# Sums of squares of eight norms: one f32 product with ones against two fp32r products of a rounded part and a rest

## The reference

```python
def rms_norm(x, g):
    xf = x.astype(jnp.float32)
    y = xf * lax.rsqrt(jnp.mean(xf * xf, axis=-1, keepdims=True) + EPS) * g.astype(jnp.float32)
    return y.astype(x.dtype)
```

## Time and profile before

| | |
|---|---|
| median of three executions | 3236.54 us |
| the profiled execution: its time | 3235.9 us |
| the profiled execution: its span | 3234.1 us |
| TensorE (PE) busy | 3172.7 us, 98% |
| TensorE weight loads (PEld) | 2582.4 us, 80% |
| VectorE (DVE) busy | 1799.1 us, 56% |
| ScalarE (ACT) busy | 1143.2 us, 35% |
| GpSimd (POOL) busy | 438.8 us, 14% |
| DMA engines, mean share | 27% |
| mean granted clock of TensorE | 0.997 of 2.4 GHz |

### The profile page before, as it was taken

One profiled execution on the slowest core, in us unless ns is written; L12 is line 12 of the kernel. 1 busy time (PEld: TensorE's weight loads), 2 busy tenths in 40 slices (PEclk: granted clock), 3 DMA queues, 4 the chain that ended last, 5 costly groups with the idle time before them and its releaser, 6 DMA issues. The chain is left out here.

```text
span 3234.1 us, 41361 instructions
## 1 busy us (share of the span) xinstructions
PE 3172.7 (98%) x15706; PEld 2582.4 (80%) x15706; DVE 1799.1 (56%) x1935; ACT 1143.2 (35%) x1330; POOL 438.8 (14%) x339
## 2 busy tenths in 40 slices
PE   8899999999999999999999999999999999999998
PEld 6678888877788888888877888888888876888887
DVE  7775535459653455544586654345444576664344
ACT  4463322249432222322353433223322343533221
POOL 2001000110100025000153120003000154120002
PEclk9999999999999999999999999999999999999999
DMA  4212232232123224222221122324223221122322
GB/s 157 80 48 76 100 104 91 103 112 72 66 91 104 91 93 116 104 95 103 86 84 53 66 91 84 111 81 126 103 91 104 78 92 66 53 91 91 104 88 81
DMA packets 46599, 293.44 MB, mean 91 GB/s; under 512 B 5888, under 2 KB 6272, under 8 KB 18336
## 3 DMA queue, kind: packets, MB, share of 16 engines
q1 hardware_dynamic: 44496, 286.97, 25.9%
q0 software_dynamic: 2000, 5.05, 1.0%
HBM read 289.24 MB, written 2.10 MB: 90 GB/s over the span
## 5 line engine op out<-in xcount | busy, mean ns | idle before, releaser
L1899 DVE TENSOR_TENSOR w_lo<-w_raw,w_hi 128x2048 fp32r<-128x2048 f32 (+1 forms) x284 | 666.7, 2348 | 242.1 <-ACT w_hi L1460 241.9
L900 PE MATMUL ps<-xg_hi,w_hi 128*128 128x512 f32 x1920 | 749.7, 390 | 2.2 <-DVE w_lo L1899 2.2
L900 PE MATMUL ps<-xg_hi,w_lo 128*128 128x512 f32 x1920 | 747.1, 389 | 0.0
L900 PE MATMUL ps<-xg_lo,w_hi 128*128 128x512 f32 x1920 | 747.0, 389 | 0.0
L1460 ACT ACTIVATE w_hi<-w_raw 128x2048 fp32r<-128x2048 f32 (+1 forms) x286 | 541.2, 1892 | 476.5 <-PE ps L900 359.5
L900 PE MATMUL ps<-hid_hi,w_hi 128*128 128x512 f32 x1216 | 473.4, 389 | 0.0
L900 PE MATMUL ps<-hid_lo,w_hi 128*128 128x512 f32 x1216 | 473.1, 389 | 0.0
L900 PE MATMUL ps<-hid_hi,w_lo 128*128 128x512 f32 x1216 | 473.1, 389 | 0.0
L900 PEld LDWEIGHTS ps<-xg_hi,w_hi 128*128 128x128 f32 x1920 | 360.4, 188 | 79.2 <-issue 4.8
L900 PEld LDWEIGHTS ps<-xg_lo,w_hi 128*128 128x128 f32 x1920 | 360.4, 188 | 75.9 <-issue 1.4
L900 PEld LDWEIGHTS ps<-xg_hi,w_lo 128*128 128x128 f32 x1920 | 360.4, 188 | 75.3
(11 more groups left out here) (362 smaller groups left out, 3933.1 us busy)
## 6 DMA issues: line engine op xcount, KB each, us to landing
w_raw<-up_dram SPq DMA_DIRECT2D x120, 1024.0 KB, 4.9
w_raw<-in_dram SPq DMA_DIRECT2D x42, 1024.0 KB, 4.9
w_raw<-down_dram SPq DMA_DIRECT2D x32, 1024.0 KB, 4.8
w_raw<-down_dram SPq DMA_DIRECT2D x32, 768.0 KB, 4.2
w_raw<-down_dram SPq DMA_DIRECT2D x32, 640.0 KB, 3.9
w_raw<-out_dram SPq DMA_DIRECT2D x14, 1024.0 KB, 4.9
w_raw<-out_dram SPq DMA_DIRECT2D x8, 768.0 KB, 4.2
w_raw<-memk_dram SPq DMA_DIRECT2D x4, 1024.0 KB, 4.9
```

What stands on the lines that cost most here:

```text
L900: last = pe.matmul(to, (w_hi, w_lo)[wp][:, q, t:t + P], parts[xp], start=(k == 0 and m == 0), stop=(k == p.ktiles - 1 and m == 2))
L1899: dve.tensor_tensor(w_lo[:, q, 0:w], w_raw[:, q, 0:w], w_hi[:, q, 0:w].bitcast(F32), ALU.subtract)\
```

## The change

GpSimd gets two more instructions behind each of the eight sums: a copy of `ssq` into an fp32r tile `ssq_hi`, which rounds, and a subtraction that leaves the rest in `ssq_lo`. `ssq_lo` lies on the bytes of `ssq`, and `ssq_hi` on those of `sq`. TensorE waits for the second of them and makes two fp32r products with ones into the same bank in place of the one f32 product. Two semaphores are added; `split_before(n)` counts how many such splits came before norm n. The first norm, the middle one and the last one stay as they were.

```diff
+def split_before(n):
+
+    return n - 1 - (n > gained(MID + 1))
...
+    ssq_lo = at("ssq_lo", [S], F32R, c[0])
     ssq = const("ssq", [S])
+    ssq_hi = at("ssq_hi", [S], F32R, c[0])
     sq = const("sq", [S])
...
+        def split_sums(n):
+
+            pool.wait_ge(ssq_ready, DT * (n + 1))
+            pool.tensor_copy(ssq_hi[:], ssq[:]).then_inc(ssq_h, 1)
+            pool.wait_ge(ssq_h, split_before(n) + 1)
+            pool.tensor_tensor(ssq_lo[:], ssq[:], ssq_hi[:].bitcast(F32), ALU.subtract).then_inc(ssq_split, 1)
...
                     pool.tensor_tensor(ssq[:], ssq[:], tmp[:, b % 2, :], ALU.add).then_inc(ssq_ready, 1)
+                split_sums(n)
...
-                    squares(n, wait, DT - 1 if p.next_norm == NORMS - 1 else DT)
+                    last = p.next_norm == NORMS - 1
+                    squares(n, wait, DT - 1 if last else DT)
+                    if not last:
+                        split_sums(n)
...
-                pe.matmul(ps[:, 7, :], ones[:], ssq[:], start=True, stop=True).then_inc(ss_mm, 1)
+                pe.wait_ge(ssq_split, split_before(n) + 1)
+                pe.matmul(ps[:, 7, :], ones[:].bitcast(F32R), ssq_hi[:], start=True, stop=False)
+                pe.matmul(ps[:, 7, :], ones[:].bitcast(F32R), ssq_lo[:], start=False, stop=True).then_inc(ss_mm, 1)
```

More of the change, by code:

```diff
@@ L336, in program @@
     ssq_ready = sem("ssq_ready")
+    ssq_h = sem("ssq_h")
+    ssq_split = sem("ssq_split")
     xsq_done = sem("xsq_done")
```

## The result

The changed kernel takes 3254.02 us (median of six executions, 3252.07 to 3257.26) against 3235.84 us (six, 3235.24 to 3236.61): 18.2 us more, a ratio of 1.0056 with a 95% interval of 1.0045 to 1.0067. The forecast was 3249.6 us, 13.1 more.

The account below looks back on a forecast made before the run. TensorE, busy 98%, was taken to bound the kernel; 12.05 + 1.83 - 0.82 = +13.1 us gave 3249.6 us. The 8-in-10 range was 3243 to 3252, the forecast's own 3247.5 to 3251, with chance 0.70.

Parts of the forecast that it names:

- TensorE saves 0.41 us a norm: At each of eight norms, two fp32r products replace one f32 product: 0.41 us saved, 3.3 us in all without waits.
- GpSimd's two instructions: Behind each sum, undisturbed: copy 0.69 us and subtraction 1.28 us, 2.13 us together with gaps.
- The copy is held behind `w_lo`: In five norms GpSimd's copy waits for VectorE's `w_lo`, lasting some 2.6 us, from 335.1 to 337.8 in up1_0_0.
- rival 1: Only GpSimd's subtraction is held by `w_lo`, not the copy: +1.65 us in five norms, +7.0 us, 3243.6 us; chance 0.13.
- The five alike: Norms up1_0_0, in1_1, in2_0, in2_1, up2_1_0_0: product 2.82 us late, less 0.41 saved, +2.41 each, +12.05 us.
- up1_1_0: At this norm the subtraction is held behind `w_lo`, so the product starts 2.24 us late, less 0.41: +1.83 us.
- the other two: Norms up2_0_1_0 and up2_1_1_0: GpSimd finishes before TensorE asks, no wait, -0.41 us each, -0.82 together.
- Whoever comes second is held: Two-input VectorE and GpSimd instructions don't run side by side; the later waits, then needs its time less some 0.13 us.
- The race in up1_1_0: GpSimd's subtraction is issued 0.1 us behind `w_lo` and held, +1.83 us; if it won, -0.24 us.
- Costed at nothing: Later root, reciprocal, evictions, slab splits and table loads add no time; a lost cover costs at most 4 us once.
- Rival 3: TensorE's later waits in attention and gated stages, 15.9 us, shrink and give the stalls back: not slower; chance 0.05.
- what TensorE is spared or made to wait there moves the end of the program one for one: Around up1_0_0's norm TensorE has no gap, at 0.227 us a slot and full clock, so delays count in full.

Follow-up runs that it names:

- e6: Kernel before with GpSimd's sums written as fp32r and two fp32r products of that one tile, no split or added wait: 3233.36 us, ratio 0.9989.
- e8: Changed kernel with the rounding copy on ScalarE instead of GpSimd, subtraction still on GpSimd: 3249.94 us, ratio 1.0038 to the kernel before.
- after: First profile of the changed kernel itself, compared with the kernel before: profiled execution 3253.88 us, median 3254.02 us.
- e9: The changed kernel, unaltered, profiled a second time: 3254.90 us.
- e10: The changed kernel, unaltered, profiled a third time: 3250.46 us.
- e2: Changed kernel plus throwaway fp32r products on TensorE ahead of its wait for the split at six norms: 3249.80 us, ratio 1.0043 to the kernel before.
- e5: Changed kernel with copy, subtraction and wait kept, but the old single f32 product of the unsplit sum: 3255.69 us, ratio 1.0063 to the kernel before.
- e4: Changed kernel with token_rms 24 products later in four norms and both in2 norms back to unsplit f32: 3238.89 us, ratio 1.0009 to the kernel before.
- e3: Changed kernel with VectorE starting the neighbouring w_lo only after GpSimd's subtraction in six norms: 3237.65 us, ratio 1.0004 to the kernel before.
- e7: Changed kernel with w_lo after GpSimd's subtraction and token_rms 6 products later, both in six norms: 3233.99 us, ratio 0.9991 to the kernel before.

## Why the prediction was wrong, step by step

- **TensorE saves 0.41 us a norm**: right; e6 has 0.34 to 0.44 at all eight.
- **GpSimd's two instructions**: the copy was taken at 0.69 us and is 0.61, the subtraction at 1.28 and is 1.26 to 1.29.
- **The copy is held behind `w_lo`**, for which the trace before had no one-input row: right, 2.55 us for 0.61 in five norms. The rule of the Trainium skill (SBUF — State Buffer, section "Who interferes with whom") is borne out for it by these rows, and e8 shows the half of it that rival 1 had priced.
- **The five alike, +2.41; up1_1_0, +1.83; the other two, -0.41**: right to within 0.06 us wherever the clock held (after, e9, e10), and to 0.14 in e2. "Whoever comes second is held, and then needs its own time less some 0.13 us" and "TensorE starts again 0.16 us after the release" were good enough to add up to hundredths.
- **The race in up1_1_0**: lost, as taken, though by 0.01 us and not 0.1: the copy, held by `xg_lo`, took 0.95 us where the forecast had 1.02. With so thin a margin the right side was luck in the forecast; the six profiles with this order of work (after, e9, e10, e2, e5, e4) all have it lost, by 0.01 to 0.02 us, and what makes it so regular is not shown.
- **Costed at nothing** (reciprocal, evictions, slab splits, table loads): right here, TensorE's other waits are unchanged. e4 shows how near the edge it is: with a reciprocal that comes some 5 us later, the steps are +1.1 us in two of the three up phases where it was tried and +0.7 in the third, where -0.4 was the saving.
- **Rival 3, that the stalls are given back**: none of it; the steps are not smaller than the stalls less the saving. Two of its readings were off: the eleven groups of waits, 15.9 us, leave out two at the end of the program (17.4 us with them), and the waits are not in the mixers alone, since 2.2 us of them are for `w_lo` in the dense phases (the row stands at e4). The kind of giving back that it had in mind does exist: in e3 and e7 a wait in the mixer took up a fall of the clock.
- **The step that failed** is in the first part: at the full clock of 2.4 GHz, "what TensorE is spared or made to wait there moves the end of the program one for one". I read the clock before the change and priced the products behind a stall by it. A product that comes 2.2 to 2.8 us late (idle of 2.0 to 2.6 us by the profile) can be followed by a fall of the clock to 1.2 GHz (0.43 us a product), which adds 1.4 to 1.7 us. In the profiled execution that is 1.67 + 1.55 + 1.62 = 4.8 us behind three norms; with the forecast's 13.1 and the 0.74 at the end of the program, which does not follow the stalls, that makes 18.7 us, and the steps add up to 18.6. In medians it is the 4.2 us between the changed kernel and e2. No rival had it, so the range ended at 3252.0, 2 us short. How many falls an execution has varies: e10, with one, took 3250.46 us and lies inside the range.

The Trainium skill (TensorE: Matmul & The Clock Gate, section "HAM oscillation — how this bites in real kernels") warns that a TensorE which waits between its products falls back to the lower clock, and has longer waits in its example than those here. The rows agree in kind, but shorter ones were enough: at the norms the clock fell only where TensorE had been idle for 1.9 us or more; elsewhere it fell in the mixers and at the end of the program, where TensorE has gaps of 0.6 to 1.8 us.

## What to carry to other kernels

Before a cheaper instruction on the bound engine is paid for with work on an idle one, take the time between the idle engine's last result and the moment it is asked for (here 1.40 us, against an estimated 2.13 undisturbed and 4.2 held), and look at what the neighbour on the shared port does just there. When a stall on a full TensorE can't be avoided, price it twice, with the clock held and with the clock fallen behind it, and put the second into the range. A product may be asked for a little later (here 6 products later at no cost, where 24 made TensorE wait for a slab), but first check what waits behind its result on the engine that makes the next slab. And when steps between landmarks differ with no change nearby, list TensorE's waits of both profiles there: that found the falls of the clock that cost time and those that didn't.

## What the runs showed of the hardware

- A GpSimd copy of 128x512 f32 to fp32r takes 0.61 us and beside a two-operand VectorE subtraction 2.55 us; ScalarE's copy of the same tile takes 0.64 us beside it.
- Idle times of 2.0 to 2.6 us on an otherwise full TensorE were followed by a fall of the granted clock in 3, 3, 1 and 3 of six cases (after, e9, e10, e5), those of 1.9 to 2.0 us in 1 of 6 (e8), of 0.55 us in none of 5 (e3), and filled with throwaway products in none of 6 (e2).
- Such a fall of the granted clock to 1.2 GHz and back added 1.4 to 1.7 us where no wait came soon behind it (1.6 in e4's mixer, away from any norm), and nothing where waits of 1.0 and 0.6 us did (e3, e7).
- Two fp32r products of 128x512 take 0.41 us less of TensorE's time than one f32 product.
